# Sample value rows by a store and four broadcast loads, and the first low half of x made earlier in the norm of the up units

## The reference

```python
h = x @ p['w_in']
u_a, q_b, k_b, v_b, q_c, k_c, v_c, g_c = jnp.split(h, list(np.cumsum(SPLITS)[:-1]), axis=-1)
...
k_dec = k * jnp.exp(lg[None, :] * (L - 1.0 - idx[:, None]))[None, :, :, None]
s = jnp.exp(lg * L)[None, :, None, None] * s + jnp.einsum('blhd,blhe->bhde', k_dec, v)
...
mix = jnp.concatenate([ya, yb, yc], axis=-1).astype(x.dtype) @ p['w_out']
x = layer_norm(ALPHA * x + mix, p['ln1_g'], p['ln1_b'])
f, conv_new = conv_ffn(x, conv_prev, p['w_up'], p['conv_w'], p['conv_b'], p['w_down'])
x = layer_norm(ALPHA * x + f, p['ln2_g'], p['ln2_b'])
```

## Time and profile before

| | |
|---|---|
| median of 3 runs | 682.66 us (682.43 to 682.69) |
| profiled execution | 682.28 us |
| its span | 680.5 us |
| PE matmuls busy | 665.8 us, 98% of the span |
| DVE busy | 561.4 us, 82% |
| ACT busy | 410.7 us, 60% |
| mean DMA rate | 177 GB/s |

### The profile page before, as it was taken

One profiled execution on the slowest core, in us unless ns is written; L12 is line 12 of the kernel. 1 busy time (PEld: TensorE's weight loads), 2 busy tenths in 40 slices (PEclk: granted clock), 3 DMA queues, 4 the chain that ended last, 5 costly groups with the idle time before them and its releaser, 6 DMA issues. The chain is left out here.

```text
span 680.5 us, 13488 instructions
## 1 busy us (share of the span) xinstructions
PE 665.8 (98%) x5096; PEld 615.9 (91%) x5096; DVE 561.4 (82%) x1185; ACT 410.7 (60%) x675; POOL 85.9 (13%) x82
## 2 busy tenths in 40 slices
PE   9999999999999999999999999999999999999994
PEld 7777887989999999999977887899899999999994
DVE  6998998989998988789489995488899898884754
ACT  5776258757775766545756433677767666663343
POOL 0000000140221211200300000005012222220011
PEclk9999999999999999999999999999999999999998
DMA  8767520846674656554365663264766545556411
GB/s 325 239 259 222 197 77 5 286 105 222 210 246 154 212 185 183 178 185 151 124 209 197 202 192 96 65 245 134 177 213 210 186 162 200 178 189 195 156 53 64
DMA packets 42098, 120.56 MB, mean 177 GB/s; under 512 B 5362, under 2 KB 14482, under 8 KB 41522
## 3 DMA queue, kind: packets, MB, share of 16 engines
q1 hardware_dynamic: 40322, 115.02, 51.4%
q0 software_dynamic: 704, 3.06, 1.9%
q10 hardware_dynamic: 1008, 1.63, 0.7%
HBM read 114.21 MB, written 5.48 MB: 176 GB/s over the span
## 5 line engine op out<-in xcount | busy, mean ns | idle before, releaser
L1475 DVE TENSOR_TENSOR w_lo<-ring,w_hi 128x1024 fp32r<-128x1024 f32 x144 | 175.6, 1221 | 45.9 <-ACT w_hi L909 44.4
L416 PE MATMUL ps<-x_hi,w_hi 128*128 128x264 f32 x672 | 191.0, 284 | 1.0 <-DVE x_lo L1427 1.0
L909 ACT CAST w_hi<-ring 128x1024 fp32r<-128x1024 f32 x144 | 150.1, 1043 | 69.3 <-PE ps L418 62.7
L417 PE MATMUL ps<-x_lo,w_hi 128*128 128x264 f32 x672 | 190.4, 283 | 0.0
L418 PE MATMUL ps<-x_hi,w_lo 128*128 128x264 f32 x672 | 190.3, 283 | 0.0
L416 PEld LDWEIGHTS ps<-x_hi,w_hi 128*128 128x128 f32 x672 | 126.5, 188 | 1.8 <-issue 1.8
L409 PE MATMUL ps<-x,ring 128*128 128x264 f32 x544 | 127.1, 390 | 0.1
L417 PEld LDWEIGHTS ps<-x_lo,w_hi 128*128 128x128 f32 x672 | 126.6, 188 | 0.0
L418 PEld LDWEIGHTS ps<-x_hi,w_lo 128*128 128x128 f32 x672 | 126.0, 187 | 0.0
L409 PEld LDWEIGHTS ps<-x,ring 128*128 128x128 f32 x544 | 101.1, 190 | 21.1 <-issue 2.6
L416 PE MATMUL ps<-hff_hi,w_hi 128*128 128x264 f32 x352 | 100.4, 285 | 0.0
(11 more groups left out here) (328 smaller groups left out, 1027.1 us busy)
## 6 DMA issues: line engine op xcount, KB each, us to landing
ring<-in_units SPq DMA_DIRECT2D x187, 512.0 KB, 3.6
kv<-in_kpool SPq DMA_DIRECT2D x32, 128.0 KB, 2.5
kv<-in_vpool SPq DMA_DIRECT2D x32, 128.0 KB, 2.4
SR<-in_sret SPq DMA_DIRECT2D x2, 1024.0 KB, 6.2
out_rsample<-SR POOLq DMA_DIRECT2D x2, 1024.0 KB, 4.7
out_kv<-hb ACTq DMA_DIRECT2D x2, 528.0 KB, 4.9
out_y<-x SPq DMA_DIRECT2D x3, 264.0 KB, 2.0
prev<-in_prev SPq DMA_DIRECT2D x2, 352.0 KB, 4.9
```

The costliest lines, as they stand in the source:

```text
L416: mm(out, wh, hi, start=start, stop=False)
L417: mm(out, wh, lo, start=False, stop=False)
L909: E.did(nc.scalar.copy(w_hi[:, split_slot(i)], ring[:, ring_slot(n)]), "w_hi")
L1475: E.did(tt(w_lo[:, slot], ring[:, ring_slot(L * UNITS + i)], w_hi[:, slot].bitcast(F32), ALU.subtract), "w_lo")
```

## The change

There are two edits, and a small third one.

1. Sample value rows. PE's `v_samples` now multiplies the last 32 columns of hb (the 24 last of the prompt and the 8 samples) for each head by the identity: 4 matmuls in a layer instead of 32, into bank 7. That gives rows of values, a token on a partition, with the samples on the last 8 partitions of each head's 32. ACT copies the 128 by 128 result to a new tile vrow and stores it in device memory (64 KB). SP waits for that store and issues four loads, one for each head, that read the eight rows 32 times over, on 32 partitions each, straight into VBC (128 KB each). SP does so right behind the load of unit 21. PE and ACT do their part after unit 16 in both layers. DVE waits for the loads instead of ACT's copy.
2. The norm of the up units. DVE makes x of slice 0 straight after the first product, then the second product and the second centring, then the low half of slice 0, and from there low halves alternate with products, each two slices behind. ACT makes the high half of the slices that DVE makes (0 and 4) before its own x, not behind it.
3. The first memset raises the semaphore eps_set in place of warm, and those who wait count one more.

```diff
@@ AT @@
-       "tails": 16, "c1": 17, "vt": 17, "glu": 18, "inner": 18, "kt": 18, "vb": 18, "values": 18, "sv": 18, "rsq": 18,
+       "tails": 16, "c1": 17, "vt": 17, "glu": 18, "inner": 18, "kt": 18, "vb": 16, "values": 18, "sv": 18, "rsq": 18,
...
-       "rt": 16, "yt": 16, "out": 17, "vb": 17, "gmean": 18, "rms": 18, "gvar": 18}]
+       "rt": 16, "yt": 16, "out": 17, "vb": 16, "gmean": 18, "rms": 18, "gvar": 18}]
@@ SP @@
                     if i < 17:
                         pages(L, "vpool", i - 13, 4)
+                    if i == N_IN + 1:
+                        sp.wait_ge(S("st_vrow"), 16 * (L + 1))
+                        for h in range(HEADS):
+                            rows = v_rows[L][32 * h + 32 - NS:32 * h + 32]
+                            sp.dma_start(VBC[32 * h:32 * h + 32], bcast(rows, [32, NS, DV], 0)).then_inc(S("ld_vb"), 16)
@@ PE @@
             def v_samples(L):
 
-                for half in range(2):
-                    bank = claim(VB_BANK[L] + half, "vbev", L, half + 1)
-                    for b in range(4):
-                        for h in range(HEADS):
-                            v = hb[:, VC + h, SEQ + 4 * half + b:SEQ + 4 * half + b + 1].to_broadcast([P, 32])
-                            ins = mm(bank[32 * h:32 * h + 32, b * DV:(b + 1) * DV], v, C["ident"], start=True, stop=True,
-                                     tile_position=(0, 32 * h))
-                    E.did(ins, "vb")
+                need(pe, "in_evac", L, VC + 4 - RAW)
+                bank = claim(7, "vbev", L, 1)
+                for h in range(HEADS):
+                    v = hb[:, VC + h, T - 32:T]
+                    ins = mm(bank[32 * h:32 * h + 32, 0:DV], v, C["ident"], start=True, stop=True,
+                             tile_position=(0, 32 * h))
+                E.did(ins, "vb")
@@ ACT @@
             def v_spread(L):
-                for half in range(2):
-                    need(act, "vb", L, half + 1)
-                    E.did(nc.scalar.copy(VBC[:, 4 * half:4 * half + 4], ps[:, VB_BANK[L] + half].rearrange("p (b e) -> p b e", b=4)),
-                          "vbev")
+                need(act, "vb", L, 1)
+                if L > 0:
+                    act.wait_ge(S("st_vrow"), 16 * L)
+                E.did(nc.scalar.copy(vrow[:], ps[:, 7, 0:DV]), "vbev")
+                E.settle()
+                act.dma_start(v_rows[L], vrow[:]).then_inc(S("st_vrow"), 16)
@@ ACT, ln_up @@
                 for p in range(0, KT, 2):
+                    if p in X_DVE:
+                        upper(p)
                     for t in (p, p + 1):
                         if t in x_act:
                             needq(act, "xn", q, t + 1)
                             E.did(f(x[:, t], z[:, t], ACT.Identity, scale=gb[:, t:t + 1],
                                     bias=gb[:, KT + t:KT + t + 1]), "xo")
-                    upper(p)
+                    if p not in X_DVE:
+                        upper(p)
                     upper(p + 1)
@@ DVE, ln_tail_up @@
-                for t in range(0, KT, 2):
+
+                def upper(t):
                     ln_xn(t)
-                    if t == 4:
-                        dve.wait_ge(S(rest[0]), rest[1])
-                    ln_xn(t + 1)
                     if t in X_DVE:
-                        needq(dve, "xn", q, t + 1)
+                        E.settle()
                         E.did(ts(x[:, t], z[:, t], g[:, t:t + 1], b[:, t:t + 1], ALU.mult, ALU.add), "xe")
-                    if t == 0:
-                        ln_center(q, 5, KT)
-                        rest = E.last
-                    else:
-                        low(t - 2)
-                        low(t - 1)
+                upper(0)
+                upper(1)
+                ln_center(q, 5, KT)
+                E.settle()
+                low(0)
+                upper(2)
+                upper(3)
+                low(1)
+                for t in range(4, KT):
+                    upper(t)
+                    low(t - 2)
                 ln_nmr(q)
@@ DVE, ret_states @@
-                need(dve, "vbev", L, 2)
+                dve.wait_ge(S("ld_vb"), 16 * HEADS * (L + 1))
```

More of the change, by code:

```diff
@@ L58 @@
 OUT_AT = [1, 2, 0, 3]
-VB_BANK = [4, 2]
 WARM = [3, 2]
@@ L208, in hybrid_step @@
         kdec = at("kdec", [P, 2, HEADS])
+        vrow = at("vrow", [P, DV])
         gam = at("gam", [P, 1])
@@ L215, in hybrid_step @@
         ps = ctx.enter_context(nc.psum_tensor("ps", [P, 8, 512], F32))
+        v_rows = [nc.dram_tensor(f"v_rows{L}", [P, DV], F32, kind="Internal").ap() for L in range(DEPTH)]
         def pv(L, name, i=0, n=1):
@@ L271, in hybrid_step @@
                 "qk": 1, "trk": 1, "kd": 1, "trv": 2, "vt": 2, "trvb": 1, "vbt": 1,
-                "vb": 2, "vbev": 2, "rin": 4, "ri": 4, "rstate": 1, "rso": 1, "srg": 1, "sr": 1, "qs": 5,
+                "vb": 1, "vbev": 1, "rin": 4, "ri": 4, "rstate": 1, "rso": 1, "srg": 1, "sr": 1, "qs": 5,
                 "rsq": 1, "otev": 1, "rot": 1, "osamp": 1, "ro": 4, "oev": 4, "gmean": 4, "gd": 4, "gsq": 4,
@@ L294, in ring_slot, with bcast @@
             return n % RING
+        def bcast(ap, shape, axis):
+            return ap.unsqueeze(axis).to_broadcast(shape)
         def sample_rows(bank, cols):
@@ L739, in warm @@
                     mm(ps[:, 7, 0:T], sq2[:, 0, 0:P], sq2[:, 0], start=True, stop=True)
-            pe.wait_ge(S("warm"), 1)
+            pe.wait_ge(S("eps_set"), 1)
             warm(WARM[0])
@@ L773, in _ @@
                         vb_transposes(L)
+                    if L == 0 and i == at_["vb"]:
+                        v_samples(L)
                     if i == at_["tails"]:
@@ L785, in _ @@
                         k_transposes(L)
-                    if L == 0 and i == at_["vb"]:
-                        v_samples(L)
                     if i == at_["values"]:
@@ L801, in _ @@
                         transposes(L)
+                    if L > 0 and i == at_["vb"]:
+                        v_samples(L)
                     if L > 0 and i == at_["out"]:
                         ret_out(L)
-                    if L > 0 and i == at_["vb"]:
-                        v_samples(L)
                     if i == at_["gmean"]:
@@ L889, in branch_done @@
             return [("cata", L, k + 1), ("catb", L, k - 1), ("catc", L, k - 3)][min(k // 2, 2)]
-        def bcast(ap, shape, axis):
-            return ap.unsqueeze(axis).to_broadcast(shape)
         @block.scalar
@@ L1130, in _ @@
             logs()
-            act.wait_ge(S("eps_set"), 5)
+            act.wait_ge(S("eps_set"), 6)
             s5_params(0, 0)
@@ L1180, in _ @@
                         sb_logs(L)
+                    if L == 0 and i == at_["vb"]:
+                        v_spread(L)
                     if i == at_["srg"]:
@@ L1196, in _ @@
                         v_tokens(L)
-                    if L == 0 and i == at_["vb"]:
-                        v_spread(L)
                     if i == at_["sv"]:
@@ L1307, in _ @@
             cp = nc.vector.tensor_copy
-            E.did(nc.vector.memset(sq2[:, 0], 0.0), "warm")
+            E.did(nc.vector.memset(sq2[:, 0], 0.0), "eps_set")
             E.did(nc.vector.memset(eps_all[:, 0:1], LN_EPS), "eps_set")
```

## The result

| | before | after |
|---|---|---|
| median | 682.54 us (682.42 to 682.69, 4 runs) | 687.66 us (687.15 to 688.85, 4 runs) |
| ratio, 95% interval | | 1.0079 [1.0066, 1.0091] |
| profiled execution | 682.28 us | 688.16 us |
| its span | 680.5 us | 686.4 us |
| PE matmuls busy | 665.8 us, 98% | 667.7 us, 97% |

A forecast was written before the change was run, and what follows sets the result against it. The prediction took TensorE, busy for 98% of the span, to bound the kernel. Its terms −0.3 + 3.2 + 0.9 gave +3.8 us: 686.1 for the profiled time, 686.4 for a median, range 683.4 to 689.8.

The forecast's parts named there:

- Layer 0, −0.3: Sample value rows in layer 0: 0.3 us gained, as most of the 1.89 us of removed matmuls had covered a wait.
- Layer 1, SP's queue, +3.2: Layer 1: SP's wait for vrow's store delays unit 22's load, so everything from the centring on is 3.2 us late.
- The 0.2 us for the VBC rows ahead of unit 22: Layer 1: 0.2 us added to unit 22's landing for 512 KB of VBC rows moving ahead on the same engines.
- The signs named for it: Layer 1: about 4 us idle before unit 22's w_hi, SP's wait some 8 us, PE idle 3 to 4 us.
- The saved PE work of layer 1 ends in a wait: Layer 1: PE's saved 1.4 us brings no gain, since it ends in PE's wait.
- The way through memory: Layer 1: VBC loads land at about 438, ahead of their reader, with vrow's store landing in 2.0 us.
- The rival that all is hidden (680.6): SP's wait in layer 1 is hidden and the kernel is faster, 680.6 us; chance 0.10.
- The norm, +0.9: Norm of the up units: first start 0.44 us sooner, lost by slice 2; 0.45 us lost per layer, 0.9 over both.
- The clock: Rival: TensorE's clock falls to half in layer 1's pause; nothing to 6.3 us, taken as 3.1 more, 689.5; chance 0.09.

The follow-up runs named there:

- the rows alone: The changed kernel with the old norm of the up units, so only the new value rows: 686.68 us, ratio 1.0058 against the kernel before.
- the sooner store: New rows, old norm; in layer 1 ACT copies and stores vrow ahead of its cast of unit 21, SP's wait as in the change: 682.68 us.
- the eight matmuls: The changed kernel with eight matmuls nobody reads behind layer 1's group means, to fill PE's pause: 686.87 us, ratio 1.0056 against the kernel before.
- the states moved: New rows, old norm, SP's wait and loads behind unit 22's ring load, layer 1's first four sample states behind the centring: 680.75 us, repeated 680.87 us.
- the kernel with the loads behind unit 22: The changed kernel with SP's wait and four loads behind the ring load of unit 22 instead of unit 21: 684.84 us, ratio 1.0031; again 686.12 us.
- the norm alone: The kernel before with only the new norm of the up units, on DVE and ACT: 684.09 us, ratio 1.0017.
- sooner store, loads behind unit 22: New rows, old norm, ACT's store ahead of its cast of unit 21, SP's wait and loads behind unit 22's ring load: 681.38 us, ratio 0.9984.

## Why the prediction was right and wrong

The forecast was 686.4 us in a range of 683.4 to 689.8. The time is 687.66, slower as said. The sum was +3.8 against the profiled 682.28; the profiled execution of after came at +5.9. What is missing is one term, the fall of the clock, which the sum had at nothing; the median is as near as it is partly by luck, since the block came out 0.5 us smaller than forecast and two of the four timed executions were 1.0 us quicker than the profiled one. (The terms given for the upper end of the range add up to 689.5, not 689.8; the time lies inside either.)

**Layer 0, −0.3: right.** From ACT's row zsb (41.56) to its first pair of cat_hi (122.19) it is 80.63 us before, and 80.62 in both kernels with only the norm changed. In the change and in all ten experiments with the new rows it is 80.36 to 80.40. The gain is 0.25 us. Most of PE's 1.89 us had indeed covered a wait: ahead of sb_values PE now idles for DVE's RI.

```profile
101.97 0.66 PE L716 MATMUL ps<-ZT,VBt 128*64 128x256 f32 x4 [1.26 <-DVE RI L1734]
```

**Layer 1, SP's queue, +3.2: right in mechanism and almost in size.** Each link of the chain, forecast and measured: store issued 432.95, 433.08; landed 434.95, 434.6; unit 22 issued 436.27, 436.39; its high half 440.0, 440.01. The landing was the one with a choice in it, and it took 1.5 us (3.1 in layer 0), less than the 2.0 of the 72 KB store in the earlier trace rows and less than the estimate of 2.15 from the Trainium skill's page DMA: Bandwidth & Descriptors, section "Anatomy of one DMA — SWDGE (gpsimd) path", which gives its figures for DMAs that GpSimd issues, as that of the earlier trace rows is, while this store goes out from ACT. Its other statement, that not the DMA engines but the issuing sequencer waits, agrees with this trace: SP issued nothing from 427.18 to 434.63. The 0.2 us for the VBC rows ahead of unit 22 was a guess that this trace bears out (3.6 us from issue to ACT's high half); with the same order it was 3.9, 4.2 and 4.3 in the traces of the rows alone, the sooner store and the eight matmuls. The block measured +2.74 at the centring and not 3.09, because the stage had come in 0.35 us later than before, which I had not carried over: without any block the centring would have been that much later. The signs named for it came true: 3.77 us of idle ahead of w_hi (about 4 expected), 7.1 us of SP's wait (some 8), 3.6 us of PE's pause (3 to 4).

**The saved PE work of layer 1 ends in a wait: right, and shown; its size by chance.** Between layer 0's cat_hi and PE's first w_out matmul of layer 1 there are 328.03 us before (122.19 to 450.22) and 326.65 with the states moved (122.42 to 449.07): 1.38 us, where the step had 1.4. With layer 0's 0.25 that is 1.6 of the 1.9 us by which that kernel beats the one before. But the two numbers are not the same thing. At the centring the gain is 2.1 us (441.69 before; 439.80 with the stage 0.23 later), and 0.7 of it goes again before w_out, where DVE waits 0.85 us for ACT's square and PE 0.47 behind DVE.

**The way through memory: right for this order alone.** "The VBC loads land at about 438, ahead of their reader" came out: the last was issued at 435.9 and took 2.7 us at most, so 438.6 at the latest, and the reader came at 442.22. It does not carry over to the kernel with the loads behind unit 22. There the store landed in 3.5 us and not 1.5, the loads went out 2.3 us later, and DVE, ready at 439.0, waited 2.0 us for them. The rival that all is hidden (680.6) set its point at store, issues and load within 3.9 us, and it was the order in the queues, not the speed of a landing, that decided: two edits of a few lines, with the norm as before, reach 680.8 and 681.4.

**The norm, +0.9: right in mechanism, a little small.** Measured 0.51 and 0.60 in the two layers of the change, together 1.1, and +1.3 with the norm alone. The first start came 0.44 us sooner relative to the stage, the forecast number; slice 2 at 154.33 + 0.17 = 154.50 (154.60 forecast), and the low half of the next unit at 157.75 + 0.17 = 157.92 (158.0 forecast). Missed was the gap of 0.2 us at slice 6.

**The clock: wrong.** It stood among the rivals with 0.09, at +3.1. The step that failed is "3.9 us is less than the 4.2 us that passed at the end before the clock moved". On it the sum had nothing for the clock. The pause was 3.6 us, shorter yet, and the clock fell. One row at the end of a span, with nothing behind it, was read as a limit below which nothing happens (and read short: by windows of 1 us the clock is full until 676 and 0.58 in the next, so it moved about 4.9 us after PE's last matmul). The runs have a fall after pauses of 3.9, 3.6, 2.1 and 1.7 us, the last two with a second one of 0.4 us close behind, and none after 2.2 and 0.4 in another execution. The size was nearer: 3.1 us by half of the 6.3 us, against 2.5 us behind the pause in the change (2.2 at w_out against before) and 1.7 behind the pause of 2.1. PE worked 6.2 us at 0.50, which by itself would lose 3.1, so a part of the loss was hidden; where, was not followed. The rule that was quoted against my choice, from the Trainium skill's page TensorE: Matmul & The Clock Gate, section "Part 1: The HAM clock gate", that the low clock is the default and only activity releases it, agrees with these traces: in the change the clock fell at 444.2, while PE stood still, and came back at 451.0, while it worked.

Still open: whether an idle queue, such as POOL's, would hold the wait and the loads as well as SP's place behind unit 22; that was not tried. Nor is it known what decides, after a pause of some 2 us, whether the clock falls.

## What to carry to other kernels

A transfer through device memory costs first what stands behind its wait in the queue that issues it, then the two landings. Three moves help: the store into idle time of its engine, the wait behind the next load that has a deadline, and the reader to where it doesn't hold up others. Here the last two turned +3.9 us into −1.9, and the first two made it −1.3, without touching the work that was saved. And a pause of TensorE in a kernel that runs at full clock should be priced at its length plus a possible fall of the clock, even if it is only 2 us; here a fall cost 1.2 to 2.5 us more, at most half of the stretch at the lower clock.

## What the runs showed of the hardware

- A store of 64 KB landed 1.5 us after its issue while the queues were quiet (layer 1 of the change), and 3.5 us after it beside one 512 KB ring load. Four loads of 128 KB each, with every row read by 32 partitions, took 2.3 to 3.0 us from issue to landing in the change, where plain loads of 128 KB took 2.4 (median); issued right behind a ring load they took 3.8 to 4.3 us (sooner store, loads behind unit 22).
- The clock fell after pauses of PE as short as 1.7 us (with 0.4 us more soon after), and in the same kernel with about 2.1 us of pause it fell in one profiled execution and not in another. The times scatter with it: 684.37 to 686.45 us with the pause, 684.31 to 684.87 with it filled.
- Filling a pause with matmuls that nothing reads keeps the clock up and costs nothing while the pause lasts. It is worth less than taking the pause away.
